# Head sums of squares: rows over the tokens on four column strips, in place of columns of ones

## The chip, the cores and the metric

The kernel runs on one core of one Trainium2 chip. The metric is device time in microseconds (us), the median of several runs. A core has TensorE (matrix products, results in PSUM), VectorE, ScalarE, GpSimd and SyncE, each with its own program, joined by semaphores. In the profile they are PE (PEld for its weight loads), DVE, ACT, POOL and SP; a name with a q (SPq, ACTq) is an engine's issuing of DMAs.

## The reference

One layer of a decoder for 256 prompt tokens and 8 sequences of 4 sample tokens (288 tokens, width 1024). Three parts matter here:

- **Mixer.** `proj = h @ w_in` gives the q, k, v rows of six heads of 128 features; a causal convolution and SiLU follow. Then `q = l2norm(q) * 128 ** -0.5` and `k = l2norm(k)`, with `l2norm(x) = x * rsqrt(sum(x * x) + 1e-6)` over a head's 128 features. A sum of squares is thus wanted for each token and each of the 12 q and k heads.
- **Delta rule.** With the scaled keys a lower triangular matrix per head and chunk is built (`k @ k.T` times decay and beta) and `I + L` is inverted; state, queries and values go through the inverse.
- **Experts.** A top-4-of-32 mixture of experts: `gu = x @ w_gu[e] + b_gu[e]`, SwiGLU, `@ w_down[e] + b_down[e]`, weighted by the gates. All is float32.

## The kernel before

**Projection units.** The mixer's projection is cut into 24 units (a unit is one 128-feature tile for all 288 tokens, eight products of 128x288 at L1054). TensorE works through them in a written order (`ITEMS`), with products of the modulation weights (`ada`, L1017) between them and, after certain units, the pieces that `after_unit` lists. ScalarE and VectorE have loops over the same units: copy, three convolution taps (L1987), SiLU. GpSimd squares each q and k tile into `sq` (L2547) and the sample tokens into `sq_s`; features lie on partitions, tokens along the row.

**Sums of squares.** `norms` (L1100) takes the key heads and two query heads after unit 14, the other four query heads after unit 20. Each product has 128 tokens of squares as the stationary operand and one column of ones as the moving one; its result is one column of `norm_sum` in PSUM, tokens on partitions, which is how VectorE uses it: `key_scales` (L2056) takes the k columns and `oeps` (L2156) the q columns.

**What follows the first sums.** `key_scales` gives the scale of the keys; `l_matrix` (L2065) makes `Lm[0]` and `Lm[1]` from the key products (L1145). ScalarE stores each to DRAM (L1683, its own DMA queue), and after its work on unit 15 reads them back as 48 blocks of 32x32 (L1687). VectorE solves the 48 triangular systems, 31 steps of two instructions (`solve`, L2087 and L2089), in pieces between its other work up to unit 21. The result goes through DRAM (L818, L402) back to the full matrices, and `level_product` (L561), after the last projection units, joins the blocks. Only behind that come the reads of the sample states, the outputs, the output projection, and the first loads of expert weights, which wait for buffers that the mixer holds.

**Weights of the mixer.** SyncE loads them in blocks of 2 MB into a ring of four places (L763); a load waits until the block that had the place is used, by `slot_used`.

**Experts.** SyncE streams the 2 MB blocks into 12 slots (L851, then L952 and L955 as slots come free). Before the first expert VectorE transposes the gate and up biases (`bguT`, L2391), then writes the counts and the order of the experts (semaphore `cum`), which ScalarE and others wait for. The rows of `b_gu` come by four DMAs (L913, semaphore `bgu_in`), those of `b_down` by four later ones (L922, semaphore `rb_in`).

Of the kernel before, what the change touches and what calls it, by code (L numbers as in the profile page):

```python
# [17 lines left out]
ALU = mybir.AluOpType  # L18
# [3 lines left out]
P = 128  # L22
# [3 lines left out]
NS = NSEQ * DSEQ  # L26
# [138 lines left out]
class Chain:  # L165
# [19 lines left out]
 wout_in wpool_in x1 x1_st x2T_ps xT_ps xTm x_in xg_ps xn xn2 y_ps y_sb z_sb cur gslot rank_b selT bgu_in  # L185
# [3 lines left out]
def build(nc, x_prompt, x_sample, c_prompt, c_sample, state_pool, state_conv, state_ssm, w_ada, b_ada,  # L189
# [11 lines left out]
    with ctx:  # L201
# [64 lines left out]
        sq_s = [DD.at(6960 + 288 * i, H * NS + P - NS) for i in range(2)]  # L266
# [186 lines left out]
        norm_sum = bank(7)[:, 448:484].rearrange("p (c h) -> p c h", c=3)  # L453
        gate_sum = bank(7)[:, 256:448]
# [159 lines left out]
        def experts_pe(pe, mm, tr):  # L614
# [84 lines left out]
            def bias_products():  # L699

                pe.wait_ge(s["gbT"], 1)
                pe.wait_ge(s["rank_b"], 1)
                pe.wait_ge(s["rb_in"], 16 * NQ)
                for c in range(2):
                    for q in range(NQ):
                        r = slice(NE * q, NE * q + NE)
                        mm(total(q, c), gT[r, span(c)], b_down_sb[r, :], start=c == 0, stop=False)
                for q in range(NQ):
                    r = slice(NE * q, NE * q + NE)
                    mm(samples_out[r, :], gT[r, span(2)], b_down_sb[r, :], start=True, stop=False)  # L710
# [38 lines left out]
        def _(sp):  # L749
# [73 lines left out]
            sp.wait_ge(s["norm_ps"], 2)  # L823
# [88 lines left out]
            for q in range(NQ):  # L912
                sp.dma_start(bgu_rows[NE * q:NE * q + NE], b_gu[0].rearrange("e (a n x) -> n e a x", a=4, n=NQ)[q]  # L913
                             ).then_inc(s["bgu_in"], 16)
# [74 lines left out]
        def _(pe):  # L989
# [110 lines left out]
            def norms(hs, i):  # L1100

                for h in hs:
                    at = QK_ORDER.index(h)
                    pe.wait_ge(s["sq"], at + 1 + (at >= 8))
                    for c in range(2):
                        mm(norm_sum[:, c, h:h + 1], sq[at % 8][:, P * c:P * c + P], ones[:, 0:1], start=True, stop=True)
                pe.wait_ge(s["sq"], (9, 14)[i])
                at = (H, 0)[i]
                mm(norm_sum[:, 2, at:at + H], sq_s[i][:, 0:P], ones[:, 0:H], start=True, stop=True)
                for h in range(H):  # L1110
                    at = (H, 0)[i] + h
                    last = mm(norm_sum[0:NS, 2, at:at + 1], sq_s[i][:, NS * h:NS * h + NS], ones[:, 0:1], start=True, stop=True)
                last.then_inc(s["norm_ps"], 1)
# [77 lines left out]
            def after_unit(u):  # L1191
# [16 lines left out]
                if u == 14:  # L1208
                    pe.wait_ge(s["dexp"], 1)
                    norms(QK_ORDER[:8], 0)  # L1210
                    pe.wait_ge(s["s_silu"], 1)
                    pe.wait_ge(s["silu_done"], 8)
                    key_products(0, None)
                    pe.wait_ge(s["poolT"], 1)
                    key_products(1, PA)
                    pe.wait_ge(s["poolT"], 2)
                    key_products(2, PB)
# [21 lines left out]
                if u == 20:  # L1239
                    pe.wait_ge(s["silu_done"], 14)  # L1240
                    pe.wait_ge(s["kv_tok"], 2)
                    query_products(1, PB)
                    pe.wait_ge(s["tu_done"], 1)
                    norms(QK_ORDER[8:], 1)
                    pe.wait_ge(s["s_silu"], 2)
                    query_products(0, None)
                if u == 21:
                    pe.wait_ge(s["kv_tok"], 3)
                    query_products(2, PA)
                    pe.wait_ge(s["qkd"], 2)  # L1250
                    transposed(0, None, QKTs, "qkdT_ps")
# [254 lines left out]
        def _(act):  # L1506
# [113 lines left out]
            for u in range(N_UNITS):  # L1620
# [52 lines left out]
                if u == 13:  # L1673
                    sample_silu(0)
                    for m in range(NU):
                        act.wait_ge(s["pool_ps"], m + 1)
                        fn(poolT[:, m, :], bank((PA, PB)[m])[:, 0:TOK], ACT.Identity, scale=vecT[:, 64 + m:65 + m]
                           ).then_inc(s["poolT"], 1)
                if u == 14:
                    for c in range(2):  # L1680
                        act.wait_ge(s["lmat"], c + 2)
                        rows_of_head = l_dram[c].rearrange("h r x -> h (r x)")[:, 0:P * P]
                        act.dma_start(rows_of_head.rearrange("h (p m) -> p h m", p=P), Lm[c]).then_inc(s["blk"], 16)  # L1683
# [193 lines left out]
            for m in range(2):  # L1877
                if m:
                    act.wait_ge(s["norm_ps"], 3)
# [11 lines left out]
        def _(v):  # L1891
# [164 lines left out]
            def key_scales():  # L2056

                v.wait_ge(s["norm_ps"], 1)
                v.wait_ge(s["kk_ps"], 1)
                own(ts(r2, norm_sum[:, :, H:2 * H], EPS, None, ALU.add))  # L2060
# [50 lines left out]
            for what, u in ITEMS:  # L2111
# [40 lines left out]
                if u == 20:  # L2152
                    solve(16, 19)
                    v.wait_ge(s["norm_ps"], 2)
                    v.wait_ge(s["qk_ps"], 2)
                    own(ts(oeps, norm_sum[:, :, 0:H], EPS * DH, EPS * EPS * DH, ALU.mult, ALU.add))  # L2156
# [233 lines left out]
            v.wait_ge(s["bgu_in"], 16 * NQ)  # L2390
# [110 lines left out]
        def _(g):  # L2501
# [3 lines left out]
            for i in range(2):  # L2505
                own(g.memset(sq_s[i], 0.0))
# [148 lines left out]
```

## Time and profile before

| | us |
|---|---|
| median of 3 runs | 1192.71 |
| lowest and highest run | 1191.97, 1194.7 |
| span of the profiled execution, first to last instruction | 1187.7 |
| median less span | 5.0 |
| TensorE matmuls busy | 1016.9 |
| VectorE busy | 399.2 |
| ScalarE busy | 172.8 |
| GpSimd busy | 123.9 |

The profiled execution has a span and no time of its own beside it; what lies around the span is taken as the 5.0 us by which the median is longer. Starts in the rows are microseconds from the span's first instruction. One float32 product stands in the trace as two MATMUL instructions, so 16 products read as x32; the text calls each a pass. PEclk 1.00 is a granted TensorE clock of 2.4 GHz, 0.50 is 1.2 GHz. A busy TensorE is not one at its peak.

### The profile page before, as it was taken

How to read it: one execution, taken by the hardware profiler on the slowest of the kernel's cores; microseconds unless marked ns; L12 is line 12 of the kernel's file. 1: busy time of each engine (PE TensorE's matmuls, PEld its weight loads, DVE VectorE, ACT ScalarE, POOL GpSimd, SP SyncE). 2: the span in 40 equal slices, each digit the busy share in tenths (PEclk: the TensorE clock that was granted, in tenths of full speed). 3: DMA queues.
4: the chain of work that ended last, by engine and by line, in shares of the span. 5: the costliest groups of instructions: out<-in, count | busy, mean ns of one | idle time of the engine just before them, and what ended most of it. 6: DMA issues, size and time to landing. Idle time of an engine off the chain costs nothing.

```text
span 1187.7 us, 31859 instructions
## 1 busy us (share of the span) xinstructions
PE 1016.9 (86%) x11942; PEld 488.6 (41%) x11943; DVE 399.2 (34%) x1163; ACT 172.8 (15%) x467; POOL 123.9 (10%) x323
## 2 busy tenths in 40 slices
PE   5999999988898688997689998998765899999874
PEld 4778768453333224332233243333212333333321
DVE  2145686863232132231122232222111223232313
ACT  3252314351011001000000011000000000001002
POOL 0140122101001010010000110011000000010100
PEclk9999999989999999999899999999988999999997
DMA  9976839999999999999999997999999999999996
GB/s 325 306 274 228 309 107 334 391 354 421 426 428 428 429 429 427 430 427 430 427 430 427 430 398 327 429 428 429 428 429 428 428 429 428 430 427 429 428 429 276
DMA packets 78102, 463.66 MB, mean 390 GB/s; under 512 B 11675, under 2 KB 31457, under 8 KB 53418
## 3 DMA queue, kind: packets, MB, share of 16 engines
q1 hardware_dynamic: 72927, 461.56, 94.6%
q10 hardware_dynamic: 5139, 1.60, 0.6%
q8 instruction: 26, 0.43, 0.1%
q14 instruction: 10, 0.08, 0.0%
HBM read 455.56 MB, written 7.57 MB: 390 GB/s over the span
## 4 chain that ended last, share of the span: by engine, by line
PE 65%; DMA 18%; DVE 7%; SPq 4%; issue 4%; ACT 1%; DVEq 1%; ACTq 0%
PE psum L673 26%; PE psum L692 14%; DMA weights<-in_w_gu 12%; PE psum L1054 5%; PE psum L648 4%; DMA work<-in_w_down 4%; SPq L952 3%; PE psum L625 3%; PE psum L642 2%; PE psum L1342 2%; PE psum L1017 2%; PE psum L1058 2%; DMA weights<-in_w_ada 1%; DMA work<-l_blocks 1%; DVE work L2443 1%
## 5 line engine op out<-in xcount | busy, mean ns | idle before, releaser
L673 PE MATMUL psum<-weights,work 128*32 128x512 f32 x2928 | 345.6, 612 | 92.5 <-DMA weights<-in_w_gu 46.8
L673 PEld LDWEIGHTS psum<-weights,work 128*32 128x32 f32 x2928 | 92.5, 111 | 311.5 <-issue 239.2
L692 PE MATMUL psum<-weights,work 128*32 128x256 f32 x2624 | 166.1, 405 | 34.3 <-DVE work L2457 31.7
L2443 DVE STREAM_TRANSPOSE work<-psum 128x256 f32<-128x256 f32 x53 | 23.8, 450 | 419.7 <-PE psum L673 416.9
L692 PEld LDWEIGHTS psum<-weights,work 128*32 128x32 f32 x2624 | 85.3, 115 | 109.5 <-issue 65.6
L1859 ACT ACTIVATE work<-work x53 | 22.1, 416 | 503.2 <-DVE work L2447 503.2
L625 PE MATMUL psum<-work 128*32 128x257 f32 (+1 forms) x1296 | 90.5, 393 | 3.2 <-ACT work L1856 3.2
L2467 DVE STREAM_TRANSPOSE work<-work 128x288 f32<-128x288 f32 x53 | 25.3, 478 | 197.0 <-PE psum L648 197.0
L1054 PE MATMUL psum<-work,weights 128*128 128x288 f32 x320 | 82.3, 413 | 0.0
L1054 PEld LDWEIGHTS psum<-work,weights 128*128 128x128 f32 x320 | 60.0, 191 | 17.9 <-issue 2.2
L625 PEld LDWEIGHTS psum<-work 128*32 128x32 f32 (+1 forms) x1296 | 38.3, 111 | 70.5 <-issue 62.1
L2595 POOL COPY work<-work 128x3 f32 x32 | 6.0, 186 | 550.9 <-issue 550.9
L673 PE MATMUL psum<-work 128*32 128x512 f32 x464 | 56.8, 607 | 6.1 <-DMA work<-in_w_gu 6.1
L648 PE MATMUL psum<-work 32*128 32x256 f32 x864 | 61.9, 399 | 0.0
L1864 ACT COPY work<-work 128x256 f32 x53 | 21.4, 404 | 249.4 <-PE psum L692 249.4
L692 PE MATMUL psum<-work 128*32 128x256 f32 x768 | 47.5, 389 | 2.4 <-DMA work<-in_w_down 2.4
L648 PEld LDWEIGHTS psum<-work 32*128 32x128 f32 x864 | 38.9, 183 | 23.5 <-issue 22.2
L2603 POOL TENSOR_TENSOR work<-work 128x96 f32<-128x96 f32 x53 | 19.2, 362 | 268.2 <-PE psum L625 268.1
L1987 DVE SCALAR_TENSOR_TENSOR weights<-psum,work,weights 128x255 f32<-128x255 f32 (+2 forms) x54 | 25.9, 480 | 34.9 <-ACT weights L1653 33.5
L642 PE MATMUL psum<-work 32*32 32x256 f32 x432 | 34.2, 386 | 1.0 <-DVE work L2470 1.0
L692 PEld LDWEIGHTS psum<-work 128*32 128x32 f32 x768 | 25.8, 114 | 21.4 <-DMA work<-in_w_down 4.3
L673 PEld LDWEIGHTS psum<-work 128*32 128x32 f32 x464 | 15.6, 111 | 43.3 <-issue 32.8
(405 smaller groups left out, 905.2 us busy)
## 6 DMA issues: line engine op xcount, KB each, us to landing
weights<-in_w_gu SPq DMA_DIRECT2D x112, 2048.0 KB, 37.0
weights<-in_w_down SPq DMA_DIRECT2D x48, 2048.0 KB, 39.9
work<-in_w_gu SPq DMA_DIRECT2D x16, 2048.0 KB, 36.8
work<-in_w_down SPq DMA_DIRECT2D x16, 2048.0 KB, 43.2
weights<-in_w_ada SPq DMA_DIRECT2D x12, 2048.0 KB, 10.9
weights<-in_w_in SPq DMA_DIRECT2D x5, 2048.0 KB, 14.8
weights<-in_w_out SPq DMA_DIRECT2D x2, 2048.0 KB, 8.2
weights<-in_state_ssm SPq DMA_DIRECT2D x8, 384.0 KB, 5.9
```

What stands on the lines that cost most here:

```text
L625: last = mm(bank(XB)[r, 0:cols], sel[r, c, :] if c == 2 else sel[:, c, :], rhs, start=c == 0, stop=c == 2)
L642: last = mm(samples_out[r, :], selT[r, 0:SLOTS], y_st[r, :], start=False, stop=end)
L648: last = mm(total(q, c), selT[r, SLOTS + P * c:SLOTS + P * c + P], y_st[r, :], start=False, stop=end and c == 1)
L673: last = mm(bank(GB)[SLOTS * n:SLOTS * n + SLOTS, :].rearrange("p (a x) -> p a x", a=4), xTm[:, k, :], gu[:, k % 2, n], start=k == 0, stop ...
L692: last = mm(bank(YB)[SLOTS * q:SLOTS * q + SLOTS, 0:QW], hT[:, k, :], dn[:, k % 4, QW * q:QW * q + QW], start=k == 0, stop=k == KT - 1)
L952: sp.dma_start(slot_gu(n), src).then_inc(s[f"w_in{n}"], 16)
L1017: last = mm(ada_out(i)[32 * j:32 * j + 32, :], cT[:, k, :], ring[at][:, k, P * j:P * j + P], start=k == 0, stop=k == KT - 1)
L1054: last = mm(out[:, 0:TOK], w[:, k, P * i:P * i + P], hT[:, k, :], start=k == 0, stop=k == KT - 1)
L1058: last = mm(out[:, 0:cols], hT[:, k, span(c)], w[:, k, 0:cols], start=k == 0, stop=k == KT - 1)
L1987: ins = stt(qkvT[:, h, sh:SEQ], ps[:, 0:SEQ - sh], vecT[:, tap:tap + 1], qkvT[:, h, sh:SEQ], ALU.mult, ALU.add)
L2443: v.transpose(features, of_slots[0]).then_inc(s["hid_step"], 1)
L2467: v.transpose(selT.rearrange("p (b t) -> p b t", b=NB), sel_blk).then_inc(s["selT"], 1)
```

## The change

`norms` goes. In its place `square_sums` makes rows: the squares become the moving operand, and the stationary one is 32 columns of `one_of`, all zeros but one column of ones, so that the sums of head n come out as one row (tokens along it) of the 32-partition strip n % 4. Eight (then four) heads share a bank of 288 columns by accumulating into their strips. ScalarE copies the bank to `head_sums` once. `sums_by_token` then turns it: 128 tokens of `head_sums` as the stationary operand, a few columns of the identity as the moving one. The order of heads in `norm_sum` changes, and with it the slices that VectorE reads; key products of the third group come after the turning, `square_sums(1)` comes ahead of the query products.

The ScalarE copy needs a semaphore. The name `bgu_in` is given up for it: the four loads of `b_gu` now count on `rb_in`, together with the four of `b_down`, and both waits on them are for all eight.

```diff
  ring1 ring2 ring3 root router_ps rr rt_in s_new s_ps s_silu s_taps sc_ps total_ps sel sel_step setup_ps
  setup_sb rk2 tt_done un_ps sig silu_done slot_used small_in softplus_a softplus_v sp_e sq ssm_in ssm_out ssq
  stats_set t0 tailT_ps tails tail_rows out_st tap3 tn_ps top_e tu_done u0 u0_ps u_sb rows_in vmask vn vn_ps
- wout_in wpool_in x1 x1_st x2T_ps xT_ps xTm x_in xg_ps xn xn2 y_ps y_sb z_sb cur gslot rank_b selT bgu_in
+ wout_in wpool_in x1 x1_st x2T_ps xT_ps xTm x_in xg_ps xn xn2 y_ps y_sb z_sb cur gslot rank_b selT nsq_sb
  bguT ahead xTa y_st curb """.split()
...
         sq = [DD.at(4144 + 256 * i, SEQ) for i in range(8)]
         s_tmp = DD.at(6192, H, NS)
         s_tap = DD.at(6384, CT, NS)
-        sq_s = [DD.at(6960 + 288 * i, H * NS + P - NS) for i in range(2)]
+        sq_s = [DD.at(6960 + 288 * i, H * NS) for i in range(2)]
+        one_of, head_sums = DD.at(7536, 2 * SLOTS), DD.at(4144 + 4 * SEQ, TOK)
         mraw = DD.at(4144, ADA_FIRST, P)
         X3 = Arena(Wt, SLOT_W, 3 * SLOT_W)
         tokK_s, valS, tokV_s, mraw_f = X3.at(0, H // 2, DH), X3.at(GW // 2, H // 2, DH), X3.at(GW, GW), X3.at(2 * GW, 4, P)
...
             return heads(pair, P)
         norm_sum = bank(7)[:, 448:484].rearrange("p (c h) -> p c h", c=3)
+        head_sums_ps = [bank(b)[:, 0:TOK] for b in (2, 0)]
+        NORM_HEADS = [H + h for h in range(H)] + list(range(H))
         gate_sum = bank(7)[:, 256:448]
         def heads(b, n, m=P):
...
                 pe.wait_ge(s["gbT"], 1)
                 pe.wait_ge(s["rank_b"], 1)
-                pe.wait_ge(s["rb_in"], 16 * NQ)
+                pe.wait_ge(s["rb_in"], 32 * NQ)
                 for c in range(2):
                     for q in range(NQ):
                         r = slice(NE * q, NE * q + NE)
...
             sp.wait_ge(s["side_st"], 128)
             sp.wait_ge(s["pool_ps"], 2)
             sp.wait_ge(s["s_silu"], 3)
-            sp.wait_ge(s["norm_ps"], 2)
+            sp.wait_ge(s["norm_ps"], 4)
             sp.wait_ge(s["tn_ps"], 1)
             sp.wait_ge(s["tails"], 1)
             for b in range(NSEQ):
...
             sp.wait_ge(s["mix_ps"], 4)
             for q in range(NQ):
                 sp.dma_start(bgu_rows[NE * q:NE * q + NE], b_gu[0].rearrange("e (a n x) -> n e a x", a=4, n=NQ)[q]
-                             ).then_inc(s["bgu_in"], 16)
+                             ).then_inc(s["rb_in"], 16)
             load(1, 2)
             store_x1(2)
             sp.wait_ge(s["side_st"], 128 + 64)
...
             half_unit(2, 0)
             half_unit(6, 0)
-            def norms(hs, i):
-
-                for h in hs:
-                    at = QK_ORDER.index(h)
+            def square_sums(i):
+
+                def add(n, cols, src, start, stop):
+                    g, r = n % 4, n // 4 - 2 * i if n // 4 - 2 * i >= 0 else 1
+                    return mm(head_sums_ps[i][32 * g:32 * g + 32, cols], one_of[:, 31 - r:63 - r], src, start=start, stop=stop)
+
+                for n in (range(8), range(8, 12))[i]:
+                    at = QK_ORDER.index(NORM_HEADS[n])
                     pe.wait_ge(s["sq"], at + 1 + (at >= 8))
-                    for c in range(2):
-                        mm(norm_sum[:, c, h:h + 1], sq[at % 8][:, P * c:P * c + P], ones[:, 0:1], start=True, stop=True)
+                    add(n, slice(NS, TOK), sq[at % 8], start=n % 8 < 4, stop=n >= 4)
                 pe.wait_ge(s["sq"], (9, 14)[i])
-                at = (H, 0)[i]
-                mm(norm_sum[:, 2, at:at + H], sq_s[i][:, 0:P], ones[:, 0:H], start=True, stop=True)
-                for h in range(H):
-                    at = (H, 0)[i] + h
-                    last = mm(norm_sum[0:NS, 2, at:at + 1], sq_s[i][:, NS * h:NS * h + NS], ones[:, 0:1], start=True, stop=True)
+                for n in ((0, 1, 2, 3, 4, 5), (8, 9, 10, 11, 6, 7))[i]:
+                    h = n % H
+                    one = n in (2, 3, 8, 9)
+                    last = add(n, slice(0, NS), sq_s[i][:, NS * h:NS * h + NS], start=n in (0, 1, 2, 3, 8, 9, 10, 11), stop=one or n in (4, 5, 6, 7))
+                last.then_inc(s["norm_ps"], 1)
+
+            def sums_by_token(i):
+
+                pe.wait_ge(s["nsq_sb"], i + 1)
+                pick = ident.rearrange("p (g x) -> p x g", g=4)
+                for c, at in enumerate((NS, NS + P, 0)):
+                    parts = ((0, 4, pick[:, 0, :]), (4, 8, pick[:, 1, :])) if i == 0 else ((8, 12, pick[:, 0, :]), (6, 8, pick[:, 1, 2:4]))
+                    for lo, hi, rows in parts[:2 if i == 0 or c == 2 else 1]:
+                        last = mm(norm_sum[:, c, lo:hi], head_sums[:, at:at + P], rows, start=True, stop=True)
                 last.then_inc(s["norm_ps"], 1)
             def gate_sums():
...
                            ).then_inc(s["pool_ps"], 1)
                 if u == 14:
                     pe.wait_ge(s["dexp"], 1)
-                    norms(QK_ORDER[:8], 0)
+                    pe.wait_ge(s["poolT"], 2)
+                    square_sums(0)
                     pe.wait_ge(s["s_silu"], 1)
                     pe.wait_ge(s["silu_done"], 8)
                     key_products(0, None)
-                    pe.wait_ge(s["poolT"], 1)
                     key_products(1, PA)
-                    pe.wait_ge(s["poolT"], 2)
+                    sums_by_token(0)
                     key_products(2, PB)
                 if u == 16:
                     pe.wait_ge(s["lmat"], 2)
...
                 if u == 20:
                     pe.wait_ge(s["silu_done"], 14)
                     pe.wait_ge(s["kv_tok"], 2)
+                    pe.wait_ge(s["kv_tok"], 3)
+                    square_sums(1)
                     query_products(1, PB)
                     pe.wait_ge(s["tu_done"], 1)
-                    norms(QK_ORDER[8:], 1)
                     pe.wait_ge(s["s_silu"], 2)
                     query_products(0, None)
+                    sums_by_token(1)
                 if u == 21:
                     pe.wait_ge(s["kv_tok"], 3)
                     query_products(2, PA)
...
                         act.wait_ge(s["pool_ps"], m + 1)
                         fn(poolT[:, m, :], bank((PA, PB)[m])[:, 0:TOK], ACT.Identity, scale=vecT[:, 64 + m:65 + m]
                            ).then_inc(s["poolT"], 1)
+                if u in (14, 20):
+                    i = (14, 20).index(u)
+                    act.wait_ge(s["norm_ps"], 2 * i + 1)
+                    act.copy(head_sums, head_sums_ps[i]).then_inc(s["nsq_sb"], 1)
                 if u == 14:
                     for c in range(2):
                         act.wait_ge(s["lmat"], c + 2)
...
             act.wait_ge(s["total_ps"], rounds)
             for m in range(2):
                 if m:
-                    act.wait_ge(s["norm_ps"], 3)
+                    act.wait_ge(s["norm_ps"], 5)
                     fn(fst[0:n, 6:7], bank(0)[0:n, 0:1], ACT.Sqrt, bias=st[0:n, 12:13]).then_inc(s["root"], 1)
                     act.wait_ge(s["fin_y"], 1)
                 for c in range(2):
...
             def key_scales():
-                v.wait_ge(s["norm_ps"], 1)
+                v.wait_ge(s["norm_ps"], 2)
                 v.wait_ge(s["kk_ps"], 1)
-                own(ts(r2, norm_sum[:, :, H:2 * H], EPS, None, ALU.add))
+                own(ts(r2, norm_sum[:, :, 0:H], EPS, None, ALU.add))
                 own(v.reciprocal(r2, r2))
                 tt(b2, beta, r2, ALU.mult).then_inc(s["rk2"], 1)
                 v.wait_ge(s["rk2"], 1)
...
                     solve(12, 16)
                 if u == 20:
                     solve(16, 19)
-                    v.wait_ge(s["norm_ps"], 2)
+                    v.wait_ge(s["norm_ps"], 4)
                     v.wait_ge(s["qk_ps"], 2)
-                    own(ts(oeps, norm_sum[:, :, 0:H], EPS * DH, EPS * EPS * DH, ALU.mult, ALU.add))
+                    own(ts(oeps, norm_sum[:, :, H:2 * H], EPS * DH, EPS * EPS * DH, ALU.mult, ALU.add))
                     qk_decayed(0, None)
                     qk_decayed(1, PB)
                     solve(19, 25)
...
             v.wait_ge(s["xg_ps"], 1)
             x_transposes()
             v.wait_ge(s["hT_a"], KT + 4)
-            v.wait_ge(s["bgu_in"], 16 * NQ)
+            v.wait_ge(s["rb_in"], 32 * NQ)
             v.transpose(bguT.rearrange("p (a j) e -> p a j e", a=4), bgu_rows.rearrange("p a (f j) -> p a j f", j=4)
                         ).then_inc(s["bguT"], 1)
             v.wait_ge(s["bguT"], 1)
...
             own = Chain(g, s["ch_pool"])
             own(g.memset(wpbd, 0.0))
             own(g.memset(uext[:, :, 0:PBUF], 0.0))
-            for i in range(2):
-                own(g.memset(sq_s[i], 0.0))
+            own(g.memset(one_of, 0.0))
+            own(g.memset(one_of[:, 31:32], 1.0))
             flat = blk_t[0:BLOCKS].rearrange("p i j -> p (i j)")
             own(g.memset(flat, 0.0))
             own(g.memset(flat[:, 0:SOLVE * SOLVE:SOLVE + 1], 1.0))
```

## Rows read from the trace of the kernel before

**Rows 1.** The page: its first line, and DMA in 40 slices of 29.7 us

```profile
span 1187.7 us, 31859 instructions
...
DMA  9976839999999999999999997999999999999996
```

**Rows 2.** Chain that ended last, 90 to 192 us: start us, us, what

```profile
101.38 3.46 PE psum L1106 x32
...
105.54 4.89 PE psum L1145 x36
...
112.32 4.09 PE psum L1054 x16
...
116.96 12.06 DMA work<-l_blocks
...
146.68 1.95 PE psum L1106 x16
...
157.18 1.34 PE psum L1152 x12
...
164.69 13.74 PE psum L1058 x32
...
178.49 0.95 PE psum L561 x47
```

**Rows 3.** Stretches of 3 us: length, PE, PEld, DVE, ACT, POOL busy, PEclk, DMA share, GB/s

```profile
106.00:109.00 3.00, 3.00 (x14) 3.00 (x15) 1.81 (x10) 0.00 (x0) 0.00 (x0) 0.50 0.03 5
...
151.00:154.00 3.00, 3.00 (x33) 2.28 (x25) 2.79 (x8) 0.00 (x0) 0.00 (x0) 0.56 0.12 10
```

**Rows 4.** Chain that ended last, a MoE round's down projection

```profile
326.42 3.59 PE psum L692 x64
```

**Rows 5.** Timeline of ScalarE, 88 to 185 us

```profile
97.63 0.91 ACT L1677 ACTIVATE work<-psum,work 128x288 f32<-128x288 f32 x2
```

**Rows 6.** Timeline of VectorE, 88 to 185 us; in brackets idle before and releaser

```profile
106.06 0.17 DVE L2060 TENSOR_SCALAR work<-psum 128x18 f32<-128x18 f32 x1 [2.47 <-PE psum L1145]
...
108.84 3.28 DVE L2069 SCALAR_TENSOR_TENSOR weights<-psum,work,weights 128x128 f32<-128x128 f32 x12 [1.03 <-PE psum L1145]
...
129.12 0.41 DVE L2087 TENSOR_TENSOR work<-work 48x31 f32<-48x31 f32 x1 [6.63 <-DMA work<-l_blocks]
...
146.29 0.33 DVE L2150 TENSOR_TENSOR weights<-weights,psum 32x192 f32<-32x192 f32 x1
...
162.38 0.95 DVE L2108 TENSOR_TENSOR weights<-psum,weights 128x768 f32<-128x768 f32 x1
```

**Rows 7.** Line L1683, its first DMA alone, issued at 110.5 us

```profile
DMA to landing us min/median/max: 2.8/2.8/2.8
```

**Rows 8.** Line L1683, its second DMA alone

```profile
L1683 ACTq DMA_DIRECT2D l_blocks<-weights x1: 389/389/389, 112.1 to 112.1; - x1
...
DMA to landing us min/median/max: 4.8/4.8/4.8
```

**Rows 9.** Timeline of SyncE's queue, 95 to 190 us

```profile
112.38 0.37 SPq L763 DMA_DIRECT2D weights<-in_w_ada  x1
```

**Rows 10.** Line L922, the loads of b_down

```profile
L922 SPq DMA_DIRECT2D work<-in_b_down x4: 421/462/504, 257.1 to 258.6; - x4
...
DMA to landing us min/median/max: 17.2/17.4/18.1
```

**Rows 11.** Timeline of VectorE, 240 to 300 us

```profile
268.79 1.11 DVE L2391 STREAM_TRANSPOSE work<-work 128x512 f32<-128x512 f32 x1
```

**Rows 12.** Timeline of TensorE, 240 to 300 us

```profile
279.08 2.15 PE L625 MATMUL psum<-work 128*32 128x257 f32 x24 [3.19 <-ACT work L1856]
```

**Rows 13.** Line L955, loads of w_down, 268 to 330 us

```profile
DMA to landing us min/median/max: 20.4/27.5/34.6
```

**Rows 14.** Waits of TensorE, 380 to 420 us: us in total, times, longest

```profile
PE psum L673 <- DMA weights<-in_w_gu: 7.3, 3, 3.0
...
PE psum L673 <- DMA work<-in_w_gu: 1.7, 1, 1.7
```

## Prediction

> **What bounds the kernel now.** I read the page first, then the chain that ended last from 90 to 192 us, then the engines' timelines there, and at the end the start of the expert stage. The page's DMA line [rows 1] is to be seen as two halves: 9s, broken by one 7, from about 270 us to the end, where the experts' weights stream, and a hole (a 3) in the sixth slice, 148 to 178 us, where the mixer works and its buffers are not yet free for expert weights. What the mixer saves can reach the end only by letting that stream start earlier.
>
> The chain before the hole [rows 2] runs through TensorE: the first sums (101.38), key products (105.54), the modulation products, unit 15 (112.32 + 4.09 = 116.41). There it passes to a DMA: ScalarE reads the blocks back at 116.96, and 12.06 us later, at 129.02, VectorE starts to solve; it had been idle for 6.63 us [rows 6]. Of the later rows of VectorE [rows 6] the ones at 146.29 and 162.38 have no bracket: no idle ahead of them. VectorE works through, and TensorE's piece after unit 20 starts as VectorE's row at 146.29 ends (146.29 + 0.33, then 146.68 in [rows 2]). So two chains run side by side, TensorE's and VectorE's from the read on, and they meet at `level_product` (178.49), which comes right behind the last projection products (164.69 + 13.74 = 178.43) [rows 2]. A gain has to be on both.
>
> The second thing to see is the clock: 0.50 for all of 106 to 109 us and a mean of 0.56 from 151 to 154 [rows 3]. TensorE counts as busy throughout. Both stretches follow a run of 128x1 products.
>
> **The change part by part.**
>
> *Sums after unit 14.* They and the key products take 101.38 to 105.54 + 4.89 = 110.43, or 9.05 us [rows 2]. New: 8 products of 256 columns on strips are 16 passes; the nearest row, 64 passes on four strips in 3.59 us [rows 4], gives 56 ns each, 0.9 us. The 6 sample products are 12 passes of 32 columns: between nothing and 56 ns each (0.67); I take 0.3. Turning: 6 products, 12 passes at the old 3.46 / 32 = 0.108 us [rows 2], 1.3 us. Key products: 12 passes of 128 columns cost 1.34 (the row of L1152) [rows 2], so groups two and three take 2.68. In the old 4.89 some 3 us ran at half speed [rows 3] and lost 1.5; 4.89 - 1.5 - 2.68 leaves 0.7 for the first group. Sum: 0.9 + 0.3 + 0.7 + 1.34 + 1.3 + 1.34 = 5.9. TensorE gains 3.2 us if the clock stays up, 1.7 if it falls as before.
>
> *ScalarE's copy.* Two copies of 128x288 took 0.91 [rows 5], so one is 0.46. Ready at 102.6, over at 103.1, while the first two groups of key products run until 104.6; it is hidden by them. Without that cover it would cost 0.5.
>
> *VectorE.* `key_scales` now waits for the turning: 101.38 + 0.9 + 0.3 + 0.7 + 1.34 + 1.3 = 105.9, against 106.06 [rows 6]: no change, as group two has been put before the turning. But the 1.03 us that `l_matrix` waited at 108.84 [rows 6] go, since its products are there. Both matrices come 1.1 us earlier.
>
> *The stores and the read.* This is where most of TensorE's gain stays. The store of `Lm[0]`, alone, landed in 2.8 us [rows 7]; that of `Lm[1]`, issued at 112.1 just ahead of a ring load (112.38) [rows 8, 9], took 4.8 and landed at 116.9, which is when the read was issued. Unit 15 and ScalarE's 0.5 us of copies ended then too. After the change unit 15 ends at 113.2, but the ring load also comes 3.2 earlier (109.2), ahead of both stores (109.4 and 111.0). Bounds for the second landing: 2.8 gives 113.8, hardly before ScalarE is free at 113.7; a wait for the first (109.4 + 4.8) and 4.8 more give 119.0. I take the row of the same situation, 4.8: 115.8, a gain of 1.1 less something for the queue, so 1.0. The Trainium skill ("Trainium Kernel Development and Optimization", Key Constraints) says that DMAs issued from different engines' queues run on the same 16 DMA engines and interleave. By that rule the dearer price holds for both stores, and the two landing rows agree; without it the gain would be 3.1.
>
> *The read* is 12.06 us [rows 2] as before: it ran beside ring loads and will again. The solve starts 1.0 earlier, and VectorE, which has no idle to give back, stays 1.0 ahead to the end of the solve.
>
> *Sums after unit 20.* Old: 16 passes in 1.95 us [rows 2] and 14 narrower ones behind. New: 8 passes of 56 ns, 0.3 for the samples, 8 turning passes of 0.108, together 1.6. TensorE gains about 1 us here, 2.5 if the clock stays up. None of it counts: TensorE, now ahead, waits for VectorE at `tu_done` and again ahead of the third group of transposes after unit 22, whose input VectorE makes at 162.38 [rows 6]. That wait is TensorE's gain less VectorE's, some 3 to 4 us in all. The last products then start and end 1.0 earlier, as the solved blocks do.
>
> *The shared semaphore.* The bias transpose, at 268.79 [rows 11], waited for the `b_gu` loads alone; now it waits for `b_down` too, which landed 17.2 to 18.1 us after issues up to 258.6 [rows 10], so at 276.7. VectorE stands still for 7.9 us. Behind it are the counts and the order of the experts, so ScalarE, and TensorE's gather at 279.08, which waited 3.19 for ScalarE already [rows 12]: TensorE is up to 7.9 late for the second half of expert 0. What hides it is the stream: the `w_down` loads that expert 0 releases landed at the earliest 20.4 us after issue [rows 13], so 7.9 later the queue still has work; and TensorE waits for weights 7.3 + 1.7 = 9.0 us between 380 and 420 [rows 14], where it makes the time up. If that cover were gone it would cost 7.9. I take nothing.
>
> The constants on GpSimd (two memsets for two) and the other waits, met long before, cost nothing.
>
> Sum, against the profiled execution: 1187.7 - 1.0 = 1186.7, and with 5.0 around it 1191.7. Bounds from the stores: -3.1 and +2.1, so 1189.6 to 1194.8.
>
> **Rivals.**
>
> *The whole gain arrives* (0.2). The second store lands as fast as one alone, and unit 15's earlier end decides: read 3.1 earlier, 1189.6. For it: the ring load, two blocks of 2 MB, would be partly through by then. Against it: the landing of 4.8 beside such a load [rows 8].
>
> *The clock falls again while TensorE waits for VectorE* (0.15). The waits worked out above sit between narrow pieces after units 20 and 22, right ahead of the 13.74 us of projection. Three microseconds at half speed there lose 1.5, so `level_product` comes 1.0 - 1.5 = 0.5 later than before: 1193.2. It decides once the loss exceeds the 1.0. The page "TensorE: Matmul & The Clock Gate" of the Trainium skill (section "Why this matters for your kernels") blames gaps between bursts of products for a falling clock; the rows of 106 to 109 show a fall without a gap, after narrow products, so gap and narrow product may both count here.
>
> *The clock falls in spite of the change* (0.1). The turning is 12 narrow passes. If the low stretch after unit 14 stays, `l_matrix` gains nothing: 1192.7.
>
> *Slower by the shared semaphore* (0.1). If TensorE's lateness exceeds the 9.0 us of waits for weights, or the stream's queue runs dry before expert 0's loads are issued, the rest is paid, at most 7.9: up to 1199.6. For it: the margin is about 1 us, and TensorE stands idle long enough for a slow clock on top. Against it: the 20.4 [rows 13].
>
> **How the numbers follow.** The forecast, TensorE gains three times what the end does, has 0.45. The time is 1191.7. Within 0.2% (2.4 us) of 1192.7, about what a measurement of this kernel can tell from no change, lie the forecast, both clock rivals, and a little of the others; below it most of the first rival and a tail of the forecast; above it the semaphore rival, where over 2.4 us of it show, and a late second store. Faster 0.23, same 0.64, slower 0.13. Range 1188.9 to 1195.0: the bounds of the stores with 0.2 to 0.7 for the spread of the runs; it leaves out most of the semaphore rival.
>
> **What would show it right or wrong.** Granted clock 1.00 from 101 to 113 us, key products over near 107; stores issued near 109.4 and 111.0 with landings of about 4.8; the read issued near 115.9; VectorE's first solve step near 128.1; a wait of TensorE for VectorE after unit 22; `level_product` near 177.5; the bias transpose some 7 us later than before, yet the first wait for weights between 380 and 420 shorter by as much. Wrong if the read starts before 114 or after 117, if the DMA share dips between 280 and 320, or if TensorE's last projection products run at the slow clock.

## The result, and the profile after

The changed kernel takes 1198.28 us (median of 22 runs, 1192.68 to 1203.44) against 1193.0 for the kernel before on the same chips: a ratio of 1.0039, interval 1.0028 to 1.005. It is slower, by 0.4%; the forecast was 1191.7, its range ended at 1195.0. Profiled executions have a time of their own here, 1.8 us above their span (1200.07 against 1198.3). By the same 1.8 the execution of [rows 1] was one of 1189.5, so the two profiles lie further apart (10.6) than the medians (5.3).

The page of the changed kernel, the line of its span and the DMA slices, as in [rows 1]:

```profile
span 1198.3 us, 31846 instructions
...
DMA  9967838999999999999999997999999999999996
```

The hole is still the sixth slice. The chain that ended last, 100 to 200 us (start us, us, what), answers to [rows 2]:

```profile
103.52 1.11 PE psum L1107 x28
104.63 1.91 PE psum L1160 x24
106.54 1.25 PE psum L1127 x12
...
112.70 13.49 DMA l_blocks<-weights
126.21 7.89 DMA work<-l_blocks
...
168.27 1.54 PE psum L1174 x6
...
170.67 14.31 PE psum L1061 x32
184.97 0.88 PE psum L564 x48
...
189.51 3.19 issue
```

Unit 14 ended at 103.5 here and at 101.4 in [rows 2]. That is no work of the change: it lies between 101.2 and 103.6 in the sixteen profiles of this study, early and late with either kind of sums. So I count from there. The sums (L1107, L1127) and key products (L1160) take less, as predicted. Then, behind VectorE's `l_matrix`, comes a *store* of 13.49 us, and only then the read. SyncE's queue, ScalarE's timeline and the landings of the stores, a fence each, answer to [rows 7 to 9]:

```profile
111.16 0.37 SPq L766 DMA_DIRECT2D weights<-in_w_ada  x1
111.58 0.58 SPq L766 DMA_DIRECT2D weights<-in_w_in  x1
```

```profile
111.15 1.94 ACTq L1704 DMA_DIRECT2D l_blocks<-weights  x2
...
126.21 0.34 ACTq L1708 DMA_DIRECT2D work<-l_blocks  x1
126.58 1.28 ACT L1711 ACT_TABLE_LOAD   x1 [10.44 <-DMA l_blocks<-weights]
```

```profile
DMA to landing us min/median/max: 8.8/11.1/13.5
```

In [rows 7 to 9] both stores (110.5, 112.1) went out ahead of the first ring load (112.38). Now the loads, 2 MB each, go out with the first store and ahead of the second (112.7), and the stores land after 8.8 and 13.5 us in place of 2.8 and 4.8. ScalarE stands 10.44 us in its wait for them and meanwhile owes TensorE the copies that come behind unit 16; TensorE waits 4.47 us for these:

```profile
131.07 1.51 PE L1182 MATMUL psum<-work,weights 128*32 128x128 f32 x24 [4.47 <-ACT weights L1584]
```

VectorE's timeline (the first solve step, then the bias transpose) answers to [rows 6, 11]:

```profile
134.20 0.20 DVE L2108 TENSOR_TENSOR work<-work 48x31 f32<-48x31 f32 x1 [4.04 <-DMA work<-l_blocks]
...
285.99 1.10 DVE L2412 STREAM_TRANSPOSE work<-work 128x512 f32<-128x512 f32 x1 [6.62 <-DMA work<-in_b_down]
```

Stretches of 3 us, the first behind unit 14 and the others at three waits of TensorE, columns as in [rows 3]; PEclk is the third number from the end:

```profile
104.00:107.00 3.00, 3.00 (x55) 2.79 (x47) 1.45 (x3) 0.88 (x3) 0.00 (x0) 1.00 0.00 0
130.00:133.00 3.00, 1.93 (x25) 1.48 (x26) 0.16 (x1) 3.00 (x9) 0.81 (x2) 0.62 0.81 208
169.00:172.00 3.00, 3.00 (x11) 2.20 (x10) 2.66 (x11) 0.00 (x0) 0.00 (x0) 0.55 0.28 67
193.00:196.00 3.00, 3.00 (x31) 2.24 (x24) 0.00 (x0) 1.43 (x5) 0.00 (x0) 0.57 0.84 284
```

And TensorE's gather of the first expert, which answers to [rows 12]:

```profile
296.26 2.95 PE L628 MATMUL psum<-work 128*32 128x257 f32 x24 [9.90 <-ACT work L1877]
```

Counted from unit 14's end the solve starts at 30.7, before at 27.7: 2.9 late, where 1.0 early was forecast. `level_product` is 4.3 late (81.4 against 77.1). Between it and the first output product 3.4 more are lost (15.1 against 11.65), in the "issue" wait of 3.19 and the half clock of 193 to 196. With the 2.1 ahead of unit 14's end and 0.6 between the outputs and the experts this is the 10.5 by which the first expert product is late (279.28 against 268.81).

### The profile page after: what moved, and what is told of

Read it like the earlier page. It is cut to its first block, busy times and chain, and to the rows that moved or that the text cites. A ratio compares the mean times of both kernels' runs of the same rounds, so it can differ in the third digit from the quotient of the medians.

```text
span 1198.3 us, 31846 instructions
## 1 busy us (share of the span) xinstructions
PE 1010.7 (84%) x11934; PEld 484.7 (40%) x11935; DVE 397.6 (33%) x1163; ACT 173.5 (14%) x469; POOL 123.5 (10%) x323
## 4 chain that ended last, share of the span: by engine, by line
PE 62%; DMA 19%; DVE 9%; issue 4%; SPq 4%; ACT 1%; DVEq 1%; ACTq 0%
PE psum L676 26%; PE psum L695 14%; DMA weights<-in_w_gu 11%; PE psum L651 4%; PE psum L1057 4%; DMA work<-in_w_down 4%; SPq L955 3%; PE psum L628 2%; PE psum L645 2%; PE psum L1359 2%; PE psum L1061 2%; DMA work<-in_b_down 2%; PE psum L1020 1%; DMA l_blocks<-weights 1%; DMA weights<-in_w_ada 1%
## 5 line engine op out<-in xcount | busy, mean ns | idle before, releaser
L695 PE MATMUL psum<-weights,work 128*32 128x256 f32 x2624 | 158.7, 391 | 37.7 <-DVE work L2478 32.2
L695 PEld LDWEIGHTS psum<-work 128*32 128x32 f32 x768 | 25.6, 112 | 20.3 <-DMA work<-in_w_down 3.5
L2609 POOL TENSOR_SCALAR work<-work 128x96 f32<-128x96 f32 x54 | 30.3, 561 | 22.0 <-PE psum L628 13.5
```

Source lines behind the costliest of these rows:

```text
L695: last = mm(bank(YB)[SLOTS * q:SLOTS * q + SLOTS, 0:QW], hT[:, k, :], dn[:, k % 4, QW * q:QW * q + QW], start=k == 0, stop=k == KT - 1)
L2609: g.tensor_scalar(selA, ahead, 0.0, None, ALU.is_equal).then_inc(s["sel"], 1)
```

## The experiments

All ratios are to the kernel before on the same chip, of five rounds, with a 95% interval. Two theories at first: the *stores behind the ring loads*, or the *shared semaphore*, whose waits of 6.62 and 9.90 are plain to see.

**The semaphore, taken out of the change and put into the kernel before.** Of the first edit the fence shows three places; the other waits on these semaphores follow. The second edit puts `rb_in`, with all eight loads on it, into the kernel before.

```diff
-                             ).then_inc(s["rb_in"], 16)
+                             ).then_inc(s["bgu_in"], 16)
...
-            v.wait_ge(s["rb_in"], 32 * NQ)
+            v.wait_ge(s["bgu_in"], 16 * NQ)
...
-                    act.copy(head_sums, head_sums_ps[i]).then_inc(s["nsq_sb"], 1)
+                    act.copy(head_sums, head_sums_ps[i]).then_inc(s["softplus_a"], 1)
```

> The change whole, but the loads of b_gu and b_down counted apart again (the copy of the sums counts on a semaphore that has done its work by then). Theory S (the stores of the key matrices stand behind two ring loads and land 8.8 and 13.5 us after issue, in place of 2.8 and 4.8): nothing comes back, about 1198, ratio 1.004. Theory B (VectorE's wait of 6.6 us for b_down is paid): all of it comes back, 1193 or below, ratio 1.000. The bias transpose follows the first x transposes at once in either case, and TensorE's gather is 6 to 7 us sooner.

> The kernel before, with the shared semaphore alone. Theory S: VectorE waits 7 to 8 us at the bias transpose, TensorE's waits for weights around 400 us shrink by as much, and the time stays at 1193, ratio 1.000. Theory B: 1198, ratio 1.004.

The first gave 1198.07, ratio 1.0035 (1.0019 to 1.005): VectorE no longer waits at the transpose, TensorE waits 3.14 instead of 9.90, and nothing is won. The second gave 1192.27, 0.999 (0.9974 to 1.0006), though VectorE stood 13.2 us and TensorE 16.6 in its profile. The semaphore is hidden. In that profile the second store was issued at 112.64, the load at 112.67, and it landed after 8.8: the order in the kernel before is a near tie. The read that followed took 8.24 in place of 12.06, so the solve started only 0.3 later there, counted from unit 14's end.

**The order, mended in the changed kernel and spoiled in the kernel before.**

```diff
             for load in LOADS[N_EARLY:]:
+                if load[:2] == ("ada", 9):
+                    sp.wait_ge(s["blk"], 32)
                 ring_load(*load)
```

> The change whole, with the ring load after unit 14 (and what is queued behind it) held until both stores of the key matrices have landed. Theory S: both stores land in about 2.8 us, the read goes out near 114 and the solve starts near 127 (after the unit 14 end of the changed kernel: 5 to 7 us sooner than there); the held load costs TensorE about 2 us of wait, so 1191 to 1194, ratio 0.998 to 1.001. Theory B: the b_down wait stays, so the time stays at 1198 or is above it for the held load.

```diff
                 if u == 14:
+                    act.wait_ge(s["slot_used"], used("ada", 8))
+                    for _ in range(4):
+                        own(act.copy(st[0:1, 14:15], st[0:1, 13:14]))
                     for c in range(2):
```

> The kernel before, with its two stores issued about 1 us later, behind the two ring loads; sums and semaphores as before. Theory S: the stores land 9 and 13 us after issue, the read goes out near 126, the solve starts 4 to 5 us later, and the time is 1196 to 1198, ratio 1.003 to 1.004. Theory B, or any theory in which the order of the queue does not matter: the delay of 1 us itself, 1194, ratio 1.001.

Held, the changed kernel takes 1191.76, 0.9979 (0.9964 to 0.9995). The kernel before with its stores about 1 us behind the first load takes 1200.41, 1.0062 (1.0043 to 1.0081), with landings of 10.0 and 15.2; the edit itself sends the two stores out 2.7 and 1.5 later, counted from unit 14's end. Of the held kernel, the landings of both stores and VectorE's first solve step:

```profile
DMA to landing us min/median/max: 2.8/2.8/2.8
```

```profile
126.37 0.20 DVE L2110 TENSOR_TENSOR work<-work 48x31 f32<-48x31 f32 x1 [7.27 <-DMA work<-l_blocks]
```

So the order alone moves either kernel, the one down and the other up, by more than the change did (0.6% against 0.4%). Two more holds of the load:

> The change whole, with the ring load after unit 14 held only until the second key matrix is made, so that it is issued at about the same time as the second store. Theory S: the order is a near tie as in the kernel before, the second store takes 4 to 9 us, the time is 1191 to 1195, ratio 0.998 to 1.002. A theory in which only the load's landing matters gives the 1198 of the change.

> The kernel before with the old sums, and the ring load held until both stores have landed, as in e3. If the new sums are worth something by themselves, this is slower than e3 by 1 to 2 us: 1193 to 1194, ratio 1.000. If all of e3's gain on the kernel before came from the order of stores and loads, it is as fast as e3: 1191 to 1192, ratio 0.998.

The first waits for `lmat` 3 in place of `blk` 32: second landing 9.1, 1193.24, 1.0002 (0.9988 to 1.0016), as expected of a tie. The second missed: the kernel before with the load held takes 1197.89, 1.0039 (1.0027 to 1.0051). There the stores went out ahead of the load already, so the hold saves little. The old sums ran at half clock for longer in its profile (0.50 from 107 to 113), the stores went out 0.9 and 1.5 later behind unit 14's end than in [rows 7, 8], and the held load 15.0 behind it, where [rows 9] have 11.0 and the held kernel with the faster sums 12.0. The read went out behind the load and took 14.34, and the solve started 31.0 behind unit 14's end, as late as in the changed kernel.

**The stores in SyncE's queue, ahead of the load, which isn't held.** ScalarE's own two stores go.

```diff
+                if load[:2] == ("ada", 9):
+                    for c in range(2):
+                        sp.wait_ge(s["lmat"], c + 2)
+                        rows_of_head = l_dram[c].rearrange("h r x -> h (r x)")[:, 0:P * P]
+                        sp.dma_start(rows_of_head.rearrange("h (p m) -> p h m", p=P), Lm[c]).then_inc(s["blk"], 16)
```

> The change whole, with the two stores issued by SyncE in its own queue right ahead of the ring load, in place of ScalarE. Theory S: they stand ahead of it in one queue, land in about 3 us, and the load need not wait for the landing, so TensorE waits some 2 us less for it than in e3: 1189 to 1191.5, ratio 0.996 to 0.999.

> The kernel before with the old sums and the two stores in SyncE's queue ahead of the ring load. Theory S: landing about 3 us each time, in place of 4.8 in one trace and 8.8 in another; 1190 to 1192.5, ratio 0.997 to 1.000, and 1 to 2 us above e8 if the new sums are worth something.

Both missed: 1193.02, 0.9999 (0.9979 to 1.0019), and 1195.19, 1.0011 (0.9994 to 1.0028). The stores landed in 2.7 and 3.3, but the read, 2.9 behind the load, took 13.6 in the changed kernel (12.95 in the held one), and TensorE still waited for `w_ada`, 1.53 and 1.25 (3.53 in the held one). With the semaphore mended as well:

> The changed kernel with the ring load held until both stores have landed, and in addition with the loads of b_gu counted on a semaphore of their own. If the shared semaphore stays hidden when the stores are quick too, this is the held kernel again: about 1191.8 us, a ratio to the kernel before of 0.997 to 0.9995, with both stores landing in 2.8 us and the experts' stream setting the end. If the late start had been covering for the shared semaphore, its own semaphore now gives something back: 1188.5 to 1190.5, below 0.997. The bias transpose comes some 6 us earlier relative to the first expert's products either way.

> The changed kernel with the two stores issued from SyncE's queue ahead of the ring load, which isn't held, and with the loads of b_gu counted on a semaphore of their own. If it is enough that the stores are quick, this and the held kernel of the same call are within 0.1% of each other, near 1192. If the read of the blocks, which here shares the DMA engines with the ring load, or the ring load itself, costs what it seemed to in the earlier run of this order, it stays at 1193, some 1.5 us above the held kernel.

1191.6, 0.9984 (0.9969 to 1.0), and 1193.99, 1.0 (0.9982 to 1.0018). The held order is again the lower by about 2 us; the intervals overlap.

**Where the rest goes: the wait put down to no semaphore.** In the held kernel `level_product` starts at 176.1, before the 178.5 of [rows 2], and yet the first expert product comes at 273.5, 4.7 later than there. In all seven profiles so far with the new sums TensorE stands still behind 46 of the 64 passes of `level_updates` (L1065 after, L1062 before), for 1.9 to 3.8 us, and runs at half clock afterwards; in all five with the old sums it stands behind 39, for 0.6 to 2.1, and the clock stays. In all twelve it is behind 1728 or 1729 passes of TensorE, counted from the start: the new sums have 8 passes fewer ahead of it. The theory is that it waits for its program. The DMA queue of instructions (q8) moves single packets of 16 KB; the changed kernel's queues from 190.1 to 191.4 us (packets, MB, share):

```profile
q1 hardware_dynamic: 738, 0.37, 113.1%
q8 instruction: 1, 0.02, 5.7%
```

From 187.5 to 190.1 it had none, the state loads had all. The packet ended at 191.4, and TensorE goes on at 192.70. The sixteen profiles show eighteen such waits of TensorE from `level_product` on, and in each it goes on 1.3 to 1.6 us after a packet of this queue has ended.

```diff
+            for _ in range(56):
+                tr(bank(2)[0:SEQS, 0:SEQS], ident[0:SEQS, 0:SEQS], ident[0:SEQS, 0:SEQS])
             pe.wait_ge(s["rows_in"], 16 * (N_VEC + N_HIST))
...
+            for _ in range(28):
+                tr(bank(4)[0:SEQS, 0:SEQS], ident[0:SEQS, 0:SEQS], ident[0:SEQS, 0:SEQS])
```

This is the padding of e11, in the held kernel. e12 has it in the changed kernel, e13 has 60 and 31 transposes in the kernel before, and e14 has 7 in the held kernel, at the first place alone.

> The changed kernel with the ring load held until the stores have landed, and 84 tiny 8x8 transposes (168 instructions, their results unused) put into TensorE's two idle stretches before 16 us. In all profiles so far TensorE stands still at its 1729th pass, for 0.6 to 2.1 us in the kernels with the old sums and for 1.9 to 3.8 us in those with the new ones, and the clock falls behind it in the new ones alone. Theory: it waits for the next 16 KB of its own program, whose transfer stands behind the state loads; the new sums have fewer instructions, so this place lies 7 passes later in the work. With 168 instructions more, that block is asked for during the last z products, ahead of the state loads: no wait within the small products, clock at 1.00 from 178 to 196 us, and 3 to 5 us less than the held kernel: 1187 to 1189. Rival: the wait belongs to the place in the work (the state loads or a buffer), not to the program: it stays behind 46 passes of the level updates, and the time at 1191.7.

> The changed kernel itself with the same 168 instructions and nothing else. If the program wait and the slow clock behind it are the second cause of the loss, beside the late stores, this wins 2 to 4 us and leaves the stores as they are: 1194 to 1196, a ratio to before of 1.001 to 1.0025. If the stores are the whole cause, it stays at 1198.

> The kernel before with 182 instructions more at the same places, so that the program's block edge falls where it does in the two padded kernels with the new sums. By the theory of the program wait it loses its wait of 0.6 to 2.1 us there and gains that at most: 1191 to 1193. If the padding itself costs or wins something (it fills idle time at the start), this shows it: a change of over 2 us here is not the wait's.

> The held kernel with 14 instructions more, so that TensorE's program wait falls behind 39 of the 64 passes of the level updates again, as in the kernel before, and not behind 46. If that place alone decides, the wait is 0.6 to 2.1 us, the clock stays up, and the time is 1187.5 to 1190. If it is the state loads, which the kernels with the new sums issue earlier against the small products, the wait goes to 39 passes but keeps 2 to 3.5 us and its slow clock, and the time stays near 1191.7. If nothing moves, the program is not what TensorE waits for.

The wait moves with the number of instructions. TensorE in the held kernel, in the one with 14 more and in the one with 168 more (two waits), a fence each:

```profile
179.19 1.51 PE L1067 MATMUL psum<-weights,work 128*32 128x128 f32 x46
184.09 1.44 PE L1067 MATMUL psum<-weights,work 128*32 128x128 f32 x18 [3.39 <-issue]
```

```profile
180.43 1.29 PE L1069 MATMUL psum<-weights,work 128*32 128x128 f32 x39
183.61 0.93 PE L1069 MATMUL psum<-weights,work 128*32 128x128 f32 x25 [1.89 <-issue]
```

```profile
180.82 0.21 PE L575 MATMUL psum<-weights,work 32*32 32x32 f32 x1 [1.32 <-issue]
...
183.96 1.32 PE L564 MATMUL psum<-weights 64*64 64x64 f32 x19
186.35 0.45 PE L564 MATMUL psum<-weights 64*64 64x64 f32 x5 [1.07 <-issue]
```

14 put it back to 39 passes. With 168 the same count of passes, 1729, falls among the 32x32 products ahead of the level updates, and TensorE stands 1.32 there; it stands again 126 passes later, among the 64x64 products. In e12 and e13 only this later wait is left. That it is the program is thus shown; why its packet comes late, behind the state loads or not, is not. With 14 and with 168 in the held kernel the clock stays at 1.00 up to 199 us, and the way from `level_product` to the outputs falls from 18.1 us to 12.4 and 13.0. What it is worth in time came out as expected in e12 alone: the changed kernel with padding takes 1196.22, 1.0021 (1.001 to 1.0033), some 2 us less than without (the intervals just overlap). The three others missed: the held one 1192.48, 0.9981 (0.9967 to 0.9994), and with 14 instructions 1192.12, 0.998 (0.9966 to 0.9993), both as without. The kernel before with padding is at 1196.47, 1.0012 (0.9996 to 1.0028): its wait went to another place, 1.77 us with a half clock behind it.

**All sixteen side by side.** The first solve step, counted from unit 14's end in each kernel's one profile, and the ratio of its median to the kernel before:

| solve starts after (us) | kernels | ratios |
|---|---|---|
| 24.8 to 25.1 | e3, e5, e11, e14 | 0.9979 to 0.9984 |
| 26.2 to 28.7 | before, e2, e6, e8, e9, e10, e13 | 0.999 to 1.0012 |
| 30.7 to 31.0 | changed kernel, e1, e7, e12 | 1.0021 to 1.0039 |
| 33.7 | e4 | 1.0062 |

A straight line through the sixteen gives 1.1 us of time for 1 us of start; e2 lies 2.2 below it, e12 1.4, the others within 1.0, and old and new sums lie on the same line. This is read from the runs; none of them moved the start of the solve and nothing else.

## Why the prediction was wrong

**Right.** The sums and key products after unit 14 took 5.6 us (103.52 to 109.15; 5.9 forecast), at a clock of 1.00 throughout. ScalarE's copy (0.40) is hidden by the key products. From unit 14's end the stores came at 7.6 and 9.2 (8.0 and 9.6 forecast), the ring load at 7.6 (7.8). The shared semaphore made VectorE stand 6.62 and TensorE 9.90, and the stream hid it, as taken; e1 and e2 show it. The wait of TensorE for VectorE after unit 22 is there (2.60 at 168.27).

**The step that failed** is *the stores and the read*. The prediction saw the load come ahead of both stores, and then took "the row of the same situation, 4.8", with an upper bound of one 4.8 after another, 119.0. It is not the same situation: in [rows 8, 9] the store went out some 0.2 us *ahead* of the load. Beside and behind the 2 MB loads the stores took 8.8 and 13.5, and from unit 14's end the read came at 22.7, where the forecast was 14.4 (115.8), the bound 17.6 and the kernel before had 15.6. "1.0 earlier" measured as 7.1 later; in the count of the rows the read came at 124.1, past the 117 that the prediction had named as a sign of being wrong. The read itself, no longer beside the loads, took 7.89 and gave 4.2 back, so the solve began 2.9 late. What was wrong was to read the price of standing behind from a row of standing in front. The price of standing behind was in the trace of the kernel before, in the landings of the two ring loads themselves (issued at 112.38 and 112.79):

```profile
DMA to landing us min/median/max: 8.4/12.2/15.9
```

The loads were forecast for 109.2 and 0.4 later, so the second of them would land at about 125.5; the second store landed at 124.1 in that count. The Trainium skill ("Trainium Kernel Development and Optimization", Key Constraints) says that DMAs of different queues interleave on the same 16 engines. The trace agrees: 2.8 us for a store alone, 8.8 and 13.5 beside the loads.

**The rivals.** *The whole gain arrives* was worked out at 1189.6, 3.1 us under the median; with the order mended (e3) 2.1 arrive by the medians and 2.5 by the ratio. *The clock falls again while TensorE waits* happened (0.55 at 169 to 172) and cost 0.6 us of z products (14.31 against 13.74), where the rival had 1.5. *Slower by the shared semaphore* had the sign by luck and not the cause.

**Not in the prediction:** the wait for the program and the clock behind it, 3.4 us in the profile, about 2 by e12, which starts its solve as late as the changed kernel (30.8 against 30.7). The order explains the larger part: mending it moves the ratio from 1.0039 to 0.9979, though in the held kernel taking the program's wait away as well brings nothing more.

**Open.** Why the 2.9 and 4.4 us that e11 and e14 win on e3 ahead of the experts in their profiles don't show in their medians. What the new sums are worth has no one answer: by e8 and e9 about 2 us, by e3 and e7 about 6, by the two padded kernels none, and the starts of the solve lie 1.7 and 6.0 earlier and 2.2 later in these pairs. By these pairs it depends on where the stores and the read fall beside the loads; no run holds that place fixed.

## What to carry to other kernels

A stage that gets faster frees buffers sooner, and the loads that wait for them then go out sooner too: list every DMA that it releases and ask which small transfer on the critical path it now overtakes. The price of a store behind a load is not the price of one in front of it; where no row shows it, the landing of the load in front is the bound to take. In the ten landings of this study with a load issued ahead of the store, or at most 0.03 us behind it, none came more than 0.3 us after the last such load's. A change of the instruction count shifts every later edge of an engine's program blocks, so a short run of tiny products can pay for an edit far ahead of it.

## What the runs showed of the hardware

- A store of 384 KB lands in 2.7 to 3.1 us alone, in 4.8 when it goes out 0.2 us ahead of two loads of 2 MB on another queue, and in 8.7 to 15.2 when it goes out together with them or up to 1.6 us behind.
- TensorE's program comes in packets of 16 KB. Where the packet came late among small products, TensorE stood 0.6 to 3.8 us and went on 1.3 to 1.6 us after the packet's end (eighteen waits of eighteen). The Trainium skill ("Runtime: NRT & Kernel Launch", Instruction fetch mechanics) has blocks of that size and calls the cost of an edge mostly hidden. Here it was not.
- A wait of TensorE of 1.9 to 3.8 us behind 46 passes was followed by a mean granted clock of 0.50 to 0.70 over the next 3 us in seven profiles of seven; so was one of 1.77 among the 64x64 products (0.73, e13). One of 1.89 behind 39 passes (e14) and one of 2.05 there (e7) were not (1.00).
